# Down stage of a hybrid decoder step: the high half of the gated activations moves from VectorE to ScalarE

## The reference, cut to what matters

```
def peer_ffn(h, w_q, sub_keys, u_tab, v_tab):
    ...
    def expert_block(args):
        hb, eb, gb = args
        act = jax.nn.gelu(jnp.einsum('td,thkd->thk', hb, u_tab[eb]).astype(f32), approximate=False)
        return jnp.einsum('thk,thkd->td', (gb * act).astype(hb.dtype), v_tab[eb])
```

## Time and profile before

| what | value |
| --- | --- |
| three executions, us | 2365.83, 2372.54, 2367.94 |
| median, us | 2367.94 |
| profiled execution, span from its first to its last instruction, us | 2380.4 |
| TensorE busy, share of that span | 98% |
| granted TensorE clock, mean | 0.996 of 2.4 GHz |

### The profile page before, as it was taken

One profiled execution on the slowest core, in us unless ns is written; L12 is line 12 of the kernel. 1 busy time (PEld: TensorE's weight loads), 2 busy tenths in 40 slices (PEclk: granted clock), 3 DMA queues, 4 the chain that ended last, 5 costly groups with the idle time before them and its releaser, 6 DMA issues.

```text
span 2380.4 us, 44269 instructions
## 1 busy us (share of the span) xinstructions
PE 2326.1 (98%) x15016; PEld 2158.8 (91%) x15016; DVE 1761.2 (74%) x3437; ACT 1078.1 (45%) x2063; POOL 934.3 (39%) x535
## 2 busy tenths in 40 slices
PE   7999899999999999999999999999999999999998
PEld 7999679998889999999999999999899999999997
DVE  8975774546647336889998988786588878787877
ACT  6554874466642224433335887886322222222222
POOL 3343465554434443444556444444332222222221
PEclk9999999999999999999999999999999999999998
DMA  3322455433144232334456998998998888898884
GB/s 130 116 79 74 138 183 185 146 106 103 61 120 134 85 119 80 121 116 148 146 163 217 324 336 329 358 340 317 399 338 310 309 298 313 290 316 296 311 294 170
DMA packets 188253, 501.40 MB, mean 211 GB/s; under 512 B 22304, under 2 KB 90944, under 8 KB 184384
## 3 DMA queue, kind: packets, MB, share of 16 engines
q1 hardware_dynamic: 72192, 229.93, 29.0%
q10 hardware_dynamic: 79072, 135.69, 15.9%
q0 software_dynamic: 36864, 134.23, 15.9%
HBM read 424.01 MB, written 76.95 MB: 210 GB/s over the span
## 4 chain that ended last, share of the span: by engine, by line
PE 77%; issue 13%; POOL 5%; DMA 2%; ACT 2%; DVE 1%; POOLq 0%; ACTq 0%; SPq 0%; DVEq 0%
PE ps L1400 26%; PE ps L807 19%; PE ps L1272 15%; POOL wlo L675 4%; PE ps L988 4%; PE ps L1358 4%; PE ps L1027 3%; DMA raw<-wt 1%; PE ps L971 1%; PE ps L1165 1%; PE ps L1117 1%; PE ps L1134 1%; PE ps L823 1%; ACT whi L1493 1%; DMA activations<-tmp 0%
## 5 line engine op out<-in xcount | busy, mean ns | idle before, releaser
L1493 ACT ACTIVATE whi<-raw 128x1024 fp32r<-128x1024 f32 x373 | 394.8, 1059 | 940.6 <-PE ps L1400 474.7
L675 POOL TENSOR_TENSOR wlo<-raw,whi 128x1024 fp32r<-128x1024 f32 x179 | 451.3, 2522 | 620.4 <-ACT whi L1493 620.4
L1272 PE MATMUL ps<-h_hi,whi 128*128 128x448 f32 x1008 | 374.5, 372 | 4.0 <-DVE wlo L2792 2.1
L1272 PE MATMUL ps<-h_hi,wlo 128*128 128x448 f32 x1008 | 368.7, 366 | 0.0
L1272 PE MATMUL ps<-h_lo,whi 128*128 128x448 f32 x1008 | 368.5, 366 | 0.0
L1400 PE MATMUL ps<-act_hi,whi 128*128 128x448 f32 x1000 | 368.0, 368 | 0.0
L1400 PE MATMUL ps<-act_lo,whi 128*128 128x448 f32 x1000 | 368.0, 368 | 0.0
L1400 PE MATMUL ps<-act_hi,wlo 128*128 128x448 f32 x1000 | 368.0, 368 | 0.0
L686 POOL DMA_INDIRECT row<-pv,row_idx x128 | 164.4, 1285 | 474.9 <-DVE row_acc L2822 455.5
L2792 DVE TENSOR_TENSOR wlo<-raw,whi 128x1024 fp32r<-128x1024 f32 x194 | 237.9, 1226 | 149.4 <-ACT whi L1493 140.2
L686 POOL DMA_INDIRECT row<-pu,row_idx x128 | 189.2, 1478 | 231.0 <-DVE row L2783 212.3
(11 more groups left out here) (386 smaller groups left out, 4688.3 us busy)
## 6 DMA issues: line engine op xcount, KB each, us to landing
raw<-wt SPq DMA_DIRECT2D x245, 512.0 KB
raw<-pv SPq DMA_DIRECT2D x128, 512.0 KB
activations<-tmp ACTq DMA_DIRECT2D x128, 224.0 KB
gates_dense<-g_block ACTq DMA_DIRECT2D x28, 1024.0 KB
g_tiles<-gates_dense ACTq DMA_DIRECT2D x32, 896.0 KB
gelu<-activations ACTq DMA_DIRECT2D x128, 224.0 KB, 5.4
a_cum_rows<-decay_sums SPq DMA_DIRECT2D x32, 256.0 KB, 3.2
state_s<-s_in SPq DMA_DIRECT2D x16, 512.0 KB, 7.1
```

Of the source, the lines that this page charges most:

```text
L675: pool.tensor_tensor(lo, raw[n.par][:, :], hi.bitcast(F32), ALU.subtract).then_inc(split_ready, 1)
L1272: mm = pe.matmul(PS[2 * p.par][:, 0:DT], w[slot][:, k, :], x[:, k, 0:DT], start=k == 0 and w is whi and x is HH, stop=k == KD - 1 and w is ...
L1493: act.activation(whi[slot][:, :, :].rearrange("p k c -> p (k c)"), raw[n.par if n.b < N_V else slot][:, :], ACT.Copy)\
```

## The change

ScalarE makes the high half of the gated activations, with a Copy of 128x448 (`act_hi`), where VectorE made it with a cast. VectorE keeps the product (`gated`), which now stands ahead of `low`, and the subtraction (`act_low`), which stands behind it and waits for ScalarE. Two new semaphores, `act_gated` and `act_high`, tell of product and high half. VectorE's own wait for tile v-4 is gone, since ScalarE's `high` has that wait ahead of `act_hi`. Three semaphores of the last part of the program are merged into others.

```
+            def act_hi(j, v):
+                act.wait_ge(act_gated, v + 1)
+                act.activation(ACH[j][:, :], GE[j][:, :], ACT.Copy).then_inc(act_high, 1)
+            for j in range(2):
+                act_hi(j, j)
             for j in range(2, 4):
                 high(Idx(N_V + j), lag=4)
+                act_hi(j, j)
...
                 load_act(j, j + 4)
                 high(Idx(N_V + 4 + j), lag=4)
+                act_hi(j, j + 4)
...
                         load_act(j, i * 8 + (8 + 4 * m + j))
                         high(Idx(N_V + 8 + 4 * m + j, i, 8), lag=4)
+                        act_hi(j, i * 8 + (8 + 4 * m + j))
...
-            def acts(b, k, n, first=False):
+            def gated(b, k, n):
                 dve.wait_ge(gated_in[b], n.quart * 32 + 32 if b == 0 else n.quart * 16 + 16)
                 ge = GE[b][:, :].rearrange("p (b t) -> p b t", b=BLOCKS)
-                own.link(dve.tensor_tensor(ge, ge, G4[k][:, :, b * TB:(b + 1) * TB], ALU.mult))
-                if not first:
-                    dve.wait_ge(tile_done, n.v - 3)
-                split(ACH[b][:, :], ACL[b][:, :], GE[b][:, :]).then_inc(act_ready, 1)
+                dve.tensor_tensor(ge, ge, G4[k][:, :, b * TB:(b + 1) * TB], ALU.mult).then_inc(act_gated, 1)
+            def act_low(b, n):
+                dve.wait_ge(act_high, n.b - N_V + n.i * n.s + 1 if n.s else n.b - N_V + 1)
+                dve.tensor_tensor(ACL[b][:, :], GE[b][:, :], ACH[b][:, :].bitcast(F32), ALU.subtract)\
+                    .then_inc(act_ready, 1)
...
                 for m in range(2):
                     for j in range(4):
                         n = Idx(N_V + 4 * m + j, i, 8)
+                        gated(j, m, n)
                         low(n)
-                        acts(j, m, n)
+                        act_low(j, n)
                         row_add(i * 8 + (4 * m + j - 4), j, i * 2 + (m - 1))
```

More of the change, by code:

```diff
@@ L462, in build @@
         picks_ready, hs_ready, hs_done = [sem(n) for n in ("picks_ready", "hs_ready", "hs_done")]
-        row_used, dots_done, dot_gelu, rows_scaled, rows_done, rows_turned = [
-            sem(n) for n in ("row_used", "dots_done", "dot_gelu", "rows_scaled", "rows_done", "rows_turned")]
+        row_used, dots_done, dot_gelu, rows_done, rows_turned = [
+            sem(n) for n in ("row_used", "dots_done", "dot_gelu", "rows_done", "rows_turned")]
         sums_ready, added, sqf_ready, tok_std = [sem(n) for n in ("sums_ready", "added", "sqf_ready", "tok_std")]
-        sq_summed, squares_summed, inv_spread, scaled, y_half = [
-            sem(n) for n in ("sq_summed", "squares_summed", "inv_spread", "scaled", "y_half")]
+        squares_summed, inv_spread, scaled, y_half = [
+            sem(n) for n in ("squares_summed", "inv_spread", "scaled", "y_half")]
         act_out = [sem(f"act_out{i}") for i in range(2)]
@@ L517, in build @@
         hot_act = sem("hot_act")
-        act_ready = sem("act_ready")
+        act_ready, act_gated, act_high = [sem(n) for n in ("act_ready", "act_gated", "act_high")]
         y_done, rinv_ready = sem("y_done"), sem("rinv_ready")
@@ L656, in _ @@
                     load_v(n, i * 4 + j)
-            sp.wait_ge(rows_scaled, 1)
+            sp.wait_ge(rows_done, 3)
             sp.dma_start(y_rows, YR[:, :]).then_inc(stored, 16)
@@ L1426, in _ @@
                 last_block(d)
-            pe.wait_ge(sq_summed, 1)
+            pe.wait_ge(added, KD + 1)
             for b in range(TN):
@@ L2848, in _ @@
             for j in range(4):
+                gated(j, 0, Idx(N_V + j))
                 low(Idx(N_V + j))
-                acts(j, 0, Idx(N_V + j), first=True)
+                act_low(j, Idx(N_V + j))
             dve.wait_ge(dot_gelu, 1)
@@ L2856, in _ @@
                 n = Idx(N_V + 4 + j)
+                gated(j, 1, n)
                 low(n)
-                acts(j, 1, n)
+                act_low(j, n)
                 row_add(j, j, 0)
             with dve.Fori(1, ET // 8) as i:
-                own.enter(i, 1, 16)
                 for m in range(2):
@@ L2864, in _ @@
                         n = Idx(N_V + 4 * m + j, i, 8)
+                        gated(j, m, n)
                         low(n)
-                        acts(j, m, n)
+                        act_low(j, n)
                         row_add(i * 8 + (4 * m + j - 4), j, i * 2 + (m - 1))
-                own.leave(ET // 8 - 1)
             for j in range(4):
@@ L2893, in _ @@
             dve.scalar_tensor_tensor(YR[:, :], ACCS[:, :], ROW_INV, FIN[:, :], ALU.mult, ALU.mult)\
-                .then_inc(rows_scaled, 1)
+                .then_inc(rows_done, 1)
             for d in (KD - 2, KD - 1):
@@ L2898, in _ @@
             own.wait()
-            dve.nop(nofuse=True).then_inc(sq_summed, 1)
+            dve.nop(nofuse=True).then_inc(added, 1)
             dve.wait_ge(std_ready, 4)
```

## The result

| | before | after |
| --- | --- | --- |
| median, us (4 runs each) | 2369.09 | 2528.88 |
| lowest to highest, us | 2365.83 to 2372.54 | 2526.51 to 2536.13 |
| span of the profiled execution, us | 2380.4 | 2528.9 |

The change makes the kernel slower: the ratio is 1.0662 [1.0629, 1.0695], 160 us. The forecast was slower, with 2403 us; the time lies 89 us above the upper end of the range.

A forecast was written before the change was run, and what follows sets the result against it. TensorE, which never waits in the down stage, was taken to bound the kernel. First seam 3.9, preparation falling behind 23.9 and last seam 7.2 sum to 35.0 us on the median 2367.9: 2403 us, range 2370 to 2440.

The forecast's parts named there:

- What bounds the kernel, and what the moved work is worth: Down stage: TensorE never waits, so VectorE's freed cast gains nothing; ScalarE's Copy, 0.55 us a tile, costs nothing.
- What is queued behind the new wait: ScalarE's next load issues only behind act_hi, exposing its landing: turns 8.57 and three of 4.07 us, 20.78 against TensorE's 19.84.
- The turn as landing plus 0.87: ScalarE's turn in the loop is the load's landing plus 0.87 us, unless VectorE's 3.82 us is longer.
- The floor of a turn: VectorE's turn in the loop falls from 4.25 to 3.82 us, the lower bound of each turn.
- The landings: Load landings in the loop: 3.2 us for three tiles of four, 7.7 for the first, with gates.
- What lead is left: Loop, tiles 12 to 124: 29 groups each lose 0.94 us, 27.3 together, less 3.4 us of lead: +23.9 us.
- The seams: Start and end of the down stage: TensorE's first tile starts late, +3.9 us; the last three tiles wait, +7.2 us.
- The clock, taken at 0: New short waits could lower TensorE's clock, up to 1.5 us each; taken as 0. As a rival 2423 us, chance 0.05.
- Loads land fast enough: Rival: four turns stay under TensorE's 19.84 us, only the first seam costs, 2372 us; chance 0.24.
- Loads land as now: Rival: landings of 5.3 us make four turns 27.1 us, 217 us lost, about 2590 us; chance 0.06.

The follow-up runs named there:

- e12: Kernel after, with SyncE loading gates about four tiles ahead, activation loads one turn ahead of the wait, VectorE casting the first four tiles: 2370.01 us, ratio 0.9985.
- e4: Kernel before, with an extra Copy of 128x448 of other data on ScalarE in 124 turns, no new wait: 2370.28 us, ratio 0.9991.
- e3: Kernel after, with the cast back on VectorE in its old place; ScalarE only waits for the product: 2503.69 us, ratio 1.0552.
- e5: Kernel after, without GpSimd's gathers of 124 of the 128 pv rows; VectorE adds the first four again and again: 2373.95 us, ratio 1.0016.
- e6: Kernel after, without the third product (low weights by high activations) in the loop, a third less TensorE work: 2529.82 us, ratio 1.066.

## Why the prediction was right or wrong

**What bounds the kernel, and what the moved work is worth: right.** VectorE's freed cast bought nothing (e12), the Copy on ScalarE took 0.58 us (0.55 forecast) and costs nothing as work (e4).

**What is queued behind the new wait: right as a mechanism.** Chain, waits and timelines show the order that was forecast, and e3 shows the wait alone to be the cause of most of it. The turn as landing plus 0.87 holds too: 6.2 + 0.87 = 7.07 against 7.15. For the gates it was 11.37 - 10.25 = 1.12, since the issue comes 0.46 us after `act_hi` starts, not 0.15. The floor of a turn, VectorE's, was 3.53 to 3.63, not 3.82.

**The landings: the step that failed.** "Preparation falls behind by 0.94 us in every four tiles" should have been 4.88, and so "What lead is left" +23.9 some 140. In the group shown the gates' turn is 2.80 us over its 8.57, one turn is 3.08 over its 4.07, and the other two are 0.44 and 0.54 under it: 20.78 + 4.90 = 25.68. From product to product the four turns of tiles 12 to 123 are 11.33, 3.63, 5.27 and 4.47 us on the mean: the gates' turn is 2.76 over its forecast and the other three together 1.16. Two choices carry that.

First, the gates, with some 70% of it. From their issue to the product it is 10.4 us on the mean of the 29 fours, where 7.7 was taken. The bounds of 6.5 and 8.6 were a guess for the groups without a wait and a mean of those with one, not the shortest and the longest; and the upper end of the range, 2440, left the gates at 7.7. The longest wait of the earlier trace rows, 3.5 us, stood there to be read. Timeline of ScalarE's queue and of VectorE in the kernel before:

```profile
2028.52 0.56 ACTq L2012 DMA_DIRECT2D g_tiles<-gates_dense  x1
...
2038.91 0.63 DVE L2830 TENSOR_TENSOR gelu<-gelu,g_tiles 128x448 f32<-128x448 f32 x1 [3.47 <-DMA gelu<-activations]
```

That is 10.39 us, the exception before and the rule after. In the kernel before TensorE spaced the turns at 4.96 us, and with them raw weights and gathers. After the change turns of 3.6 us follow one another and then stop. That the streams thereby gather round the gates is argued from the windows above; e3 and e4, with the gathers and with slower turns, fit it (6.8 and 6.3 us against 8.5). That it needs the gathers is shown by e5.

Second, a median stood for a mixture. The 3.2 that the issues show after the change is no hit: it counts every fourth load, which stands behind gates and takes 9.6 us on the mean. The three in four that were forecast at 3.2 have a median of 2.6, a mean of 3.5 and a spread from 2.3 to 6.5. A short landing can't repay a long one: below 2.7 us (3.6 - 0.87) VectorE's floor takes over.

**The seams.** The first came as worked out, 3.85 against 3.9. By the clock time the matmul is not later (1730.30 against 1730.25): in this execution TensorE was done with the stage ahead at 1726.45, and in the profiles of all runs that end lies between 1726.4 and 1734.8, so only the wait shows the seam. The last was 3.43 against 7.2. Tile 124 started at 2487.89 and TensorE's wait began at 2498.57 - 3.43 = 2495.14, so it took 7.25 us and not 4.96, at the lower clock, and covered 2.3 us of the wait. The three turns behind it took 10.68 us (products at 2485.45 and 2496.13) and not 12.21, which is the other 1.5.

**The clock, taken at 0: right in effect, wrong in fact.** It did fall, to a mean of 0.91 in the stage, as TensorE waited more than was forecast; but e6 shows that nothing in the loop waited for it.

**The rivals.** "Loads land fast enough" was decided at landings of 16.4 us in four turns. The group shown has 10.25 + 2.5 + 6.2 + 2.5 = 21.5, so it was not near. e5 is the case in which it holds: the four come to 14.7 on the mean there, and its 2374 us stand beside the 2372 forecast for it. "Loads land as now" gave 2590, nearer than the forecast in time, but that is luck: it takes 5.3 for every load without gates, where the mean is 3.5, and 7.7 for the gates.

## What to carry to other kernels

When an engine gets a new wait, list what it issues behind that wait, transfers first: a transfer issued there has its whole landing exposed in each turn, however little work was moved. Don't price that landing from a trace in which it was hidden and paced by another engine, and don't let a median stand for it: take the spread, ask what the other streams will do when the pace changes, and let the range go at least as far as the longest landing seen. The cure is to issue ahead of the wait by more than the longest landing, or from a queue whose engine doesn't have that wait; here it took one for the loads and the other for the gates.

## What the runs showed of the hardware beyond that

The same 224 KB landed in 2.5 us with the DMA engines at 0.45 to 0.58, and in 6.2 with them at 0.85. TensorE's granted clock fell with waits of a few us: the window from 2114 to 2120 us above stands at 0.50, which is 1.2 GHz, and TensorE's timeline shows a wait of 3.71 us there.

```profile
2114.78 0.74 PE L1400 MATMUL ps<-act_hi,whi 128*128 128x448 f32 x1 [3.71 <-DVE act_lo L2845]
```
